# Two elementwise steps of a gated recurrence on GpSimd instead of VectorE, in quarters

## The reference

```python
def lru_coeffs(u2, p):
    uh = uf.reshape(bn, n, 2, N_LRU_HEADS, LRU_HEAD_DIM)
    gr = einsum("bnkhi,khij->bnkhj", uh, w_r)      # 8 heads of 128, 2 directions
    gi = einsum("bnkhi,khij->bnkhj", uh, w_i)
    r, i = sigmoid(gr + b_r), sigmoid(gi + b_i)
    a = exp(-LRU_C * r * softplus(-lam))
    return a, sqrt(-expm1(2 * log_a)) * (i * uf)   # i * uf is one of the two steps

def even_mixer(h, h0, p):                          # z = h @ w_in, split into va, vg, ga, xb, gb
    y_a = silu(layernorm(depthwise_conv(va * sigmoid(vg), 31 taps))) * silu(ga)
    u = depthwise_conv(xb, 4 taps)                 # then h_t = a_t h_(t-1) + bx_t, both directions
    y_b = (forward scan + backward scan) * silu(gb)
    return concatenate([y_a, y_b]) @ p["w_out"], hT
```

## Time and profile before

| | us |
|---|---|
| median of 3 runs (lowest to highest) | 3256.74 (3254.31 to 3262.19) |
| the profiled execution | 3259.94 |
| its span | 3258.0 |
| PE busy | 2992.2 (92%) |
| DVE busy | 1779.4 (55%) |
| POOL busy | 1276.4 (39%) |
| ACT busy | 1088.9 (33%) |

### The profile page before, as it was taken

The page is one execution under the profiler, slowest core; times in us unless marked ns, Lnnn a source line. Parts: engine busy times, 40 slices in busy tenths (PEclk is TensorE's granted clock), DMA queues, the critical chain, the costliest instruction groups (busy, mean ns, idle before and its releaser), DMA issues.

```text
span 3258.0 us, 40033 instructions
## 1 busy us (share of the span) xinstructions
PE 2992.2 (92%) x13898; PEld 2302.8 (71%) x13898; DVE 1779.4 (55%) x2308; ACT 1088.9 (33%) x1414; POOL 1276.4 (39%) x1546
## 2 busy tenths in 40 slices
PE   5999999978999998989799999998999999998997
PEld 2788777756778786867688887776676666665775
DVE  4599999974354316353723322435456555556353
ACT  4343354423120000001332222223455556665332
POOL 0344444446735433436423323775212112111575
PEclk7899999989999999999899999999999999998999
DMA  9111122254311231113311012233322112111323
GB/s 378 58 66 61 61 65 68 69 194 149 106 40 48 70 125 39 48 34 126 105 38 33 26 39 97 93 89 123 59 46 46 39 40 46 47 39 40 130 81 112
DMA packets 101656, 258.46 MB, mean 79 GB/s; under 512 B 24513, under 2 KB 25601, under 8 KB 99985
## 3 DMA queue, kind: packets, MB, share of 16 engines
q1 hardware_dynamic: 71824, 189.43, 19.6%
q10 hardware_dynamic: 29696, 67.21, 5.7%
HBM read 223.97 MB, written 32.64 MB: 79 GB/s over the span
## 4 chain that ended last, share of the span: by engine, by line
PE 62%; DVE 17%; issue 9%; ACT 6%; POOL 4%; DMA 1%; DVEq 1%; SPq 0%; POOLq 0%; ACTq 0%
PE ps L579 16%; PE ps L580 15%; PE ps L581 15%; DVE ps L1936 4%; POOL t_wl L537 3%; PE ps L1068 2%; DVE t_tt L1881 1%; PE ps L1085 1%; POOL t_wh L532 1%; PE ps L882 1%; PE ps L883 1%; PE ps L884 1%; DVE t_pr L2395 1%; DVE t_pb L2154 1%; PE ps L1105 1%
## 5 line engine op out<-in xcount | busy, mean ns | idle before, releaser
L579 PE MATMUL ps<-t_h_hi,t_wh 128*128 128x512 f32 x2464 | 1018.9, 414 | 76.8 <-POOLq L540 38.8
L532 POOL CAST t_wh<-t_wst 128x1024 fp32r<-128x1024 f32 (+2 forms) x306 | 333.1, 1089 | 1840.5 <-PE ps L581 1653.6
L580 PE MATMUL ps<-t_h_lo,t_wh 128*128 128x512 f32 x2464 | 984.4, 400 | 0.0
L581 PE MATMUL ps<-t_h_hi,t_wl 128*128 128x512 f32 x2464 | 983.5, 399 | 0.0
L537 POOL TENSOR_TENSOR t_wl<-t_wst,t_wh 128x256 fp32r<-128x256 f32 (+2 forms) x1224 | 937.0, 796 | 24.5
L579 PEld LDWEIGHTS ps<-t_h_hi,t_wh 128*128 128x128 f32 x2464 | 471.3, 191 | 226.5 <-issue 99.4
L581 PEld LDWEIGHTS ps<-t_h_hi,t_wl 128*128 128x128 f32 x2464 | 469.9, 191 | 115.8
L580 PEld LDWEIGHTS ps<-t_h_lo,t_wh 128*128 128x128 f32 x2464 | 471.2, 191 | 113.7 <-issue 9.7
L1936 DVE SCALAR_TENSOR_TENSOR ps<-t_upad,t_vec,ps 128x1024 f32<-128x1024 f32 x224 | 274.6, 1283 | 6.6 <-DVE ps L1930 0.8
L579 PE MATMUL ps<-t_y_hi,t_wh 128*128 128x512 f32 x512 | 208.7, 408 | 25.3 <-DVEq L264 14.6
L581 PE MATMUL ps<-t_y_hi,t_wl 128*128 128x512 f32 x512 | 205.1, 401 | 0.0
(11 more groups left out here) (342 smaller groups left out, 4255.9 us busy)
## 6 DMA issues: line engine op xcount, KB each, us to landing
t_modw<-w_mod SPq DMA_DIRECT2D x12, 2048.0 KB, 11.6
t_wst<-w_even_in SPq DMA_DIRECT2D x40, 512.0 KB, 3.5
t_wst<-w_ple SPq DMA_DIRECT2D x64, 320.0 KB, 2.8
t_wst<-w_even_out SPq DMA_DIRECT2D x32, 512.0 KB, 3.6
t_wst<-w_fox_in SPq DMA_DIRECT2D x32, 512.0 KB, 3.6
t_xr<-x_d ACTq DMA_DIRECT2D x6, 2048.0 KB, 12.0
t_wst<-w_gla_in SPq DMA_DIRECT2D x24, 512.0 KB, 3.8
t_wst<-w_odd_in_a SPq DMA_DIRECT2D x16, 512.0 KB, 3.6
```

What stands on the lines that cost most here:

```text
L532: pool.tensor_copy(wh[b][:, 0:w], wst[b][:, 0:w]).then_inc(S("w_high"), 1)
L579: pe.matmul(o, w1, x1, start=start and k == 0, stop=False)
L580: pe.matmul(o, w1, x2, start=False, stop=False)
L581: last = pe.matmul(o, w2, x1, start=False, stop=stop and k == kts - 1)
```

## The change

GpSimd gets a function `recurrence(h)`, called after the split of each head's sixth tile (ga). It computes the low part of the result of the head before (not in the first head) in four instructions of 256 columns, and then `ii` times `u` in four instructions of 320 columns for each direction. VectorE's steps `times_u` and `low` go away; `drive` waits for the new semaphore `e_iu`. ScalarE waits for it too, before it overwrites `u` for the next head. The stream of this stage on GpSimd is written out for the first head pair and loops over the other three.

```diff
+        def recurrence(h, first_head=False):
+            if not first_head:
+                pool.wait_ge(S("e_yh"), h)
+                for q in range(4):
+                    c = slice(q * T // 4, (q + 1) * T // 4)
+                    ins = pool.tensor_tensor(yb_lo[:, c], yb[:, c], yb_hi[:, c].bitcast(F32), ALU.subtract)
+                ins.then_inc(S("e_yl"), 1)
+            for d in range(2):
+                pool.wait_ge(S("e_evac"), 8 * h + 12 + 2 * d)
+                for q in range(4):
+                    c = slice(q * TC // 4, (q + 1) * TC // 4)
+                    ins = pool.tensor_tensor(ii[d][:, c], ii[d][:, c], u[:, c], ALU.mult)
+                ins.then_inc(S("e_iu"), 1)
         for name, times, widths in STREAMS:
+            if name == "w_even_in":
+                for j, w in enumerate(widths):
+                    split_tile(name, 0, j, w, widths, 0)
+                    if j % 6 == 5:
+                        recurrence(j // 6, j == 5)
+                with pool.Fori(0, times - 1) as i:
+                    for j, w in enumerate(widths):
+                        split_tile(name, i + 1, j, w, widths, 0)
+                        if j % 6 == 5:
+                            recurrence(2 * i + 2 + j // 6)
+                continue
...
                 act.wait_ge(S("yb_stored"), 32 * i + 32)
+                act.wait_ge(S("e_iu"), 2 * i + 2)
...
-        def times_u(h, i):
-            for d in range(2):
-                line.go(TT_(ii[d][:, :], ii[d][:, :], u[:, :], ALU.mult))
-        def low(h, i):
-            if i is not None:
-                dve.wait_ge(S("e_yh"), i + 1)
-                TT_(yb_lo[:, :], yb[:, :], yb_hi.bitcast(F32), ALU.subtract).then_inc(S("e_yl"), 1)
...
         def drive(h, i):
             line.sync()
             for d in range(2):
+                dve.wait_ge(S("e_iu"), 2 * h + d + 1)
                 dve.wait_ge(S("e_sqrt"), 2 * h + d + 1)
...
-        LRU_AT = {7: times_u, 12: low, 18: q, 28: drive}
+        LRU_AT = {18: q, 28: drive}
...
+            dve.wait_ge(S("e_yl"), 7)
             TT_(col(h_lo, 7), yb[:, :], col(h_hi, 7).bitcast(F32), ALU.subtract).then_inc(S("e_yl"), 1)
...
-        line.repeat(6, 6 + 4 + 1 + 1 + TAPS + 4, lambda i: even_head(i, LRU_AT))
-        even_head(6, {7: times_u, 12: low, 18: q, 23: last_result, 26: last_low})
+        line.repeat(6, 6 + 4 + 1 + 1 + TAPS + 2, lambda i: even_head(i, LRU_AT))
+        even_head(6, {18: q, 23: last_result, 26: last_low})
```

## The result

| | before | after |
|---|---|---|
| median of 4 runs each (lowest to highest) | 3259.47 (3254.31 to 3262.93) | 3238.73 (3232.64 to 3240.67) |
| the profiled execution | 3259.94 | 3232.64 |
| its span | 3258.0 | 3230.5 |
| DVE busy | 1779.4 | 1740.6 |
| POOL busy | 1276.4 | 1303.4 |

The ratio is 0.9934 with the interval [0.9914, 0.9955]: the change makes the kernel faster by 14.7 to 28.0 us, 20.7 by the medians. Forecast were 19.56 us and 3237.2.

What follows compares the result with a forecast made beforehand. VectorE was taken to set the heads' pace, with TensorE's 66.26 us as floor. Gates 9.87 us earlier and VectorE's shorter last head end the convolution 19.56 us earlier: 3256.74 - 19.56 = 3237.2 us, range 3230 to 3252.

Steps and rivals of the forecast that it cites:

- What bounds the heads: In the eight heads, VectorE sets the pace, 68.5 to 68.6 us a head from the fourth on; TensorE waits for others.
- TensorE's own pace as the floor: Without VectorE's lag all heads run at the second head's 66.26 us; the last head's gates start 9.87 us earlier.
- the rival by which the pace stays: In the heads, the change does nothing to the pace; only the last head's 4.06 us come, 3252.7 us; chance 0.07.
- the one by which VectorE is held: In the heads, GpSimd's pieces delay VectorE beyond its spare 1.8 us; about 11 us gained, 3246 us; chance 0.13.
- VectorE's need: Per head, VectorE needs 68.6 - 4.06 = 64.5 us after the removal, less than TensorE's 66.26.
- VectorE's last head: From L1921 to the convolution's end 56.35 us instead of 60.41; it ends at 657.53, 19.56 us earlier.
- The loads shift with the convolution: Behind the last head, ScalarE issues the loads at 632.95 instead of 652.51, 19.56 us earlier, like the convolution's end.
- The rival by which the gain is given back: At the output projection, only TensorE's shift of 10.8 us or less counts, around 8: 3249 us; chance 0.08.
- GpSimd's added work: Per head 9.96 us on GpSimd, at worst 18.2, beside taps; slack 4.2 us ahead of TensorE, cost nothing.
- When GpSimd would be late: Rival for xb's split: TensorE waits 6.4 us a head, 3276.8 us; decides from 17.5 us of new work; chance 0.10.
- The sum: Whole kernel: 19.56 us saved, profiled execution 3259.94 to 3240.4 us, median 3237.2 us.
- One of my signs of being wrong: Behind the heads, a stretch from 677 us on that is longer than before would show the forecast wrong.

Runs made afterwards that it cites:

- gb first: The kernel before, with the silu of gb on ScalarE moved ahead of the store that waits for `yb_lo`: 3259.82 us, ratio 1.0002.
- the low part alone: The kernel before with only the low part of each head's result moved to GpSimd, `ii` times `u` staying on VectorE: 3254.52 us, ratio 0.9983.
- the products alone: The kernel before with only `ii` times `u` moved to GpSimd, the low part staying on VectorE: 3241.37 us, ratio 0.9942.
- the work left out: The changed kernel without GpSimd's twelve new instructions a head, only their semaphores counted: 3233.78 us, ratio 0.9914.
- Four more: The changed kernel with four more products of 320 columns a head on GpSimd, into a spare tile, behind its twelve: 3252.39 us, ratio 0.9981.
- the second series: The changed kernel without edit, timed again in 5 rounds beside the kernel before: 3236.30 us, ratio 0.9923 [0.9910, 0.9935].

## Why the prediction was right

- **What bounds the heads: right.** VectorE set the pace. gb first took TensorE's wait for the silu away, and the pace fell only by the 0.3 us that VectorE's own work was shorter; the low part alone took 0.87 us net off VectorE, and the pace went from 68.55 to 67.68.
- **TensorE's own pace as the floor: right.** 66.27 us in every head from the second on, and the products alone, the low part with them and the work left out all end on it. The reading that carried this was the second head of the kernel before, which had the same instructions without VectorE's lag. That refutes the rival by which the pace stays, and the one by which VectorE is held.
- **VectorE's need: right side, too high.** I took 64.5 us a head, with 1.8 to spare. It was busy 61.12 and had 3.2 us of air, since the 1.3 us that its other instructions lost beside GpSimd fell away too; no term stood for them. It changes nothing in the forecast, since TensorE sets the pace either way.
- **VectorE's last head: right.** 56.47 us for 56.35, started behind the gates as forecast.
- **The loads shift with the convolution: right,** 19.4 us each. The rival by which the gain is given back needed one of the two to stay.
- **GpSimd's added work: right that it costs nothing, its size a little high.** 9.19 us for 9.96, slack 5.1 for 4.2. I took a product's quarter for a subtraction's, 0.89 us; it took 0.84, and the low part's 0.61, for 0.71.
- **When GpSimd would be late: too high.** I put the point from which the rival decides at 17.5 us of new work, and held the slack for free up to 14.2. Four more is 12.95 us of work and already costs 1.1 us of wait and 1.4 us of pace a head, because its end pushes the split into `q`. I had the stretched quarter in the rows (1.30 beside `q`) and used it as a price for the new work alone, not for the split behind it. The margin was thus thinner than the rival's working said; the forecast stood on the right side of it. By its own times the split of xb ended at 229.0 and `q` came at 229.6, 0.6 us apart; measured are 1.3. That the two don't meet rests on so little, and the forecast hadn't priced it. That rival's price of 6.4 us a head left out the clock, too.
- **The sum.** 19.4 us in the trace for 19.56. The medians give 20.7 and again 23.7, and the interval of the second series (21.2 to 29.3 us) lies above 19.4. A few us may thus come from the change outside the heads. The traces can't show it: behind the heads single executions vary by some 10 us. One of my signs of being wrong, a longer stretch behind the convolution, even appeared in the second profile of the changed kernel (2583.3 us for 2580.9) and not in the first (2575.1).

On the two places where I set the Trainium skill beside the rows: the trace shows that the taps keep their time beside GpSimd's new work (eleven in 13.21 us, with it or without), while a product, a scan or `q`, with two SBUF inputs, and GpSimd's piece slow each other (2.44 to 4.97 us, 0.71 to 1.32 a piece). With the rule of the Trainium skill, SBUF — State Buffer, "SBUF: two separate sides", by which GpSimd and a VectorE instruction with two SBUF inputs lock each other out for a whole instruction, the trace agrees as to which instructions slow each other; whether one waits for the whole of the other it leaves open. By the Trainium skill, GPSIMD Engine Reference, "4.1 Engine selection", the work belongs on VectorE; this trace agrees on the durations (9.19 us for 4.06) and not on the conclusion.

## What to carry to other kernels

Where two engines are nearly equally busy, look for a stretch of the same kernel in which one of them doesn't yet hold the other back: its pace is the floor to count with, and a saving is worth only the difference to it, plus whatever the last pass alone saves. An operation may move to an engine that is half as fast if that engine waits anyway, at a place where the other runs instructions that it doesn't slow. Before the slack behind it is called free, see what the moved work pushes the next instruction into.

## What the runs showed of the hardware

- **The same four matmuls took 1.42 or 2.80 us.** The sums for the layer norm, from the first's start to the start of the next matmul, took 1.42 us in the profiled execution after (behind a wait of 3.3 us, granted clock 1.00, TensorE's 2.4 GHz) and 2.80 us in the one before (behind 4.3 us, clock 0.50, 1.2 GHz). It isn't the change: the second profile of the changed kernel has 2.79 at 0.50, behind a wait of 3.3 us as well.
- **Both sides pay when they meet.** With `q` GpSimd's quarters of 256 columns went from 0.71 to 1.32 us while `q` went from 2.89 to 3.57; a cast on GpSimd from 1.04 to 3.30 with `q` unchanged at 2.89. Which of the two gives way isn't settled by these runs.
